# The recurrence's right-hand sides by halves of heads, its masks on an earlier signal, its group norm begun inside its last steps, and the gated merge kept in PSUM

## The reference

```python
def step(state, inp):                      # per head, per token
    r_t, w_t, k_t, v_t, kk_t, a_t = inp
    sa = jnp.einsum('bhij,bhj->bhi', state, -kk_t)
    state = (state * w_t[:, :, None, :] + sa[..., None] * (kk_t * a_t)[:, :, None, :]
             + v_t[..., None] * k_t[:, :, None, :])
    y = jnp.einsum('bhij,bhj->bhi', state, r_t)
...
mean = jnp.mean(y, -1, keepdims=True)      # group norm over each head's 64 values
var = jnp.mean(jnp.square(y - mean), -1, keepdims=True)
y = ((y - mean) * lax.rsqrt(var + LNX_EPS)).reshape(B, S, RWKV_WIDTH) * lnx_g + lnx_b
y = (y + bonus) * (jax.nn.sigmoid(gl) @ g2)
...
merged = jax.nn.sigmoid(p_ga) * (y_a @ w_up_a) + jax.nn.sigmoid(p_gb) * (y_b @ w_up_b)
h = _layer_norm(DEEPNORM_ALPHA * h + merged @ w_out, ln1_g, ln1_b)
```

## Time and profile before

| | us |
|---|---|
| runs before: median (3 runs, 3464.66 to 3469.29) | 3468.47 |
| the profiled execution's own time | 3464.38 |
| its span | 3462.6 |
| PE busy in the span | 3305.0 (95%) |
| recurrence, from the first scores' masks to the last `ry` | 1874.0 to 2009.8 |
| group norm and gates, to the first up pass | 2009.8 to 2043.9 |
| up projection, to the first pass of `s.out` | 2043.9 to 2072.6 |

### The profile page before, as it was taken

The page is one execution under the profiler, slowest core; times in us unless marked ns, Lnnn a source line. Parts: engine busy times, 40 slices in busy tenths (PEclk is TensorE's granted clock), DMA queues, the critical chain, the costliest instruction groups (busy, mean ns, idle before and its releaser), DMA issues. The chain is left out here.

```text
span 3462.6 us, 40970 instructions
## 1 busy us (share of the span) xinstructions
PE 3305.0 (95%) x17376; PEld 2653.1 (77%) x17376; DVE 1335.4 (39%) x1942; ACT 1203.5 (35%) x1816; POOL 1330.1 (38%) x555
## 2 busy tenths in 40 slices
PE   8889999999999999999999879999999999999998
PEld 6678788887687788877777757888678778878886
DVE  8963421214434411222357453001374261133733
ACT  4443422224443322234434223222344432242332
POOL 4744244444253344433252013444334324414443
PEclk9999999999999999999999989999999999999999
DMA  4232122222132222223122022222222212202231
GB/s 155 80 104 86 55 98 97 98 98 91 55 116 79 72 96 96 97 91 106 55 94 92 3 90 84 97 95 94 91 98 98 80 49 95 94 31 98 98 122 67
DMA packets 83005, 302.48 MB, mean 87 GB/s; under 512 B 9060, under 2 KB 10888, under 8 KB 81928
## 3 DMA queue, kind: packets, MB, share of 16 engines
q1 hardware_dynamic: 78368, 280.55, 24.3%
q10 hardware_dynamic: 4456, 19.33, 1.5%
HBM read 290.39 MB, written 9.44 MB: 87 GB/s over the span
## 5 line engine op out<-in xcount | busy, mean ns | idle before, releaser
L3140 POOL TENSOR_TENSOR WL<-RW,WH 128x1024 fp32r<-128x1024 f32 x527 | 1294.4, 2459 | 2105.7 <-ACT WH L269 2105.2
L274 PE MATMUL PS<-XH,WH 128*128 128x512 f32 x2968 | 1169.9, 394 | 49.3 <-DVE XL L932 15.7
L275 PE MATMUL PS<-XL,WH 128*128 128x512 f32 x2968 | 1160.6, 391 | 0.0
L276 PE MATMUL PS<-XH,WL 128*128 128x512 f32 x2968 | 1160.1, 391 | 0.0
L269 ACT ACTIVATE WH<-RW 128x1024 fp32r<-128x1024 f32 x527 | 553.6, 1053 | 804.3 <-PE PS L276 698.6
L274 PEld LDWEIGHTS PS<-XH,WH 128*128 128x128 f32 x2968 | 560.5, 189 | 186.4 <-POOL WL L3140 34.0
L276 PEld LDWEIGHTS PS<-XH,WL 128*128 128x128 f32 x2968 | 560.4, 189 | 117.6
L275 PEld LDWEIGHTS PS<-XL,WH 128*128 128x128 f32 x2968 | 560.9, 189 | 116.8 <-issue 2.2
L274 PE MATMUL PS<-YH,WH 128*128 128x512 f32 (+1 forms) x928 | 351.2, 378 | 16.1 <-POOL WL L3140 7.4
L275 PE MATMUL PS<-YL,WH 128*128 128x512 f32 (+1 forms) x928 | 349.7, 377 | 0.0
L276 PE MATMUL PS<-YH,WL 128*128 128x512 f32 (+1 forms) x928 | 349.4, 377 | 0.0
(11 more groups left out here) (523 smaller groups left out, 3115.4 us busy)
## 6 DMA issues: line engine op xcount, KB each, us to landing
RW<-in_units SPq DMA_DIRECT2D x527, 512.0 KB, 3.3
spill<-X ACTq DMA_DIRECT2D x2, 2048.0 KB, 7.4
X<-in_xT SPq DMA_DIRECT2D x8, 256.0 KB, 5.8
A<-spill ACTq DMA_DIRECT2D x1, 2048.0 KB, 7.9
X<-spill ACTq DMA_DIRECT2D x4, 512.0 KB, 6.6
X<-spill ACTq DMA_DIRECT2D x1, 2048.0 KB, 7.9
out_T<-X ACTq DMA_DIRECT2D x4, 512.0 KB, 3.0
spill<-X ACTq DMA_DIRECT2D x1, 1536.0 KB, 5.1
```

The lines of the kernel that those rows point to most:

```text
L274: mm(out, hi, xh, start=first, stop=False)
L275: mm(out, hi, xl, start=False, stop=False)
L276: return mm(out, lo, xh, start=False, stop=last)
L3140: nc.gpsimd.tensor_tensor(WL[:, u % SPLIT, :], RW[:, u % RAW, :], WH[:, u % SPLIT, :].bitcast(F32), ALU.subtract).then_inc(split_done, 1)
```

## The change

- **Right-hand sides by halves.** `b0`, `b1`, `b2` are each made and signalled as two halves of two heads, in two banks; DVE's `q0`, `q1`, `q2` become two instructions of 128 x 256 each, and the next product of a half waits for that half alone. `turn` waits by halves too.
- **Masks sooner.** The scores are written in another order, first those that `D`, `DT`, `O` and the first half of `RB` need, signalled as `ab`; the others and the transposes follow. DVE's first four masks wait for `ab`. ACT's second copy of step 1 waits for `d2t` and no longer for `w`; for this the names `D` and `K` change places.
- **`y.in` in two parts.** The half of the first chunk (`within(0)`) follows `u.mm` of the second chunk, the other half stays in step 13. `y` uses banks 3 and 1.
- **Group norm begun in the second stream's tail.** In group 1's last steps PE also makes two means and all four gate products, DVE centres two tiles and applies gain, bias and gate to them, ACT squares them. The load of the gate's weights is issued half a tile earlier.
- **The rest of the norm.** The variance is made in two pairs, between passes of gate 7; the spread factors stand between passes too. DVE multiplies in PSUM (`scaled`, `biased`), and each tile is split as soon as it is done. A small Sqrt is issued on ACT ahead of the wait for the variance.
- **Up and merge.** The first round goes tile by tile as the splits arrive. Each round signals its first half alone (`up.first`), the merged tiles stay in PSUM, and hi and lo are made from there, one tile behind. `s.out` waits for the lo parts of its banks' tiles only.

The diff, cut to its core:

```diff
-        def quarters(out, L, R, w=64):
-
-            for n in range(4):
+        def quarters(out, L, R, w=64, heads=range(4)):
+
+            for n in heads:
                 for r in halves:
...
-                            mm(o, T(j)[b, tok], AR[j][b, t, :, halves[c]], start=True, stop=True)
+                            last = mm(o, T(j)[b, tok], AR[j][b, t, :, halves[c]], start=True, stop=True)
+                st.do(last, i + ".ab")
+                for q in range(2):
+                    j = 2 * g + q
...
-                st.do(quarters(bank(B + 3), F, RHS[g], P), i + ".b0")
+                st.do(quarters(bank(B + 3), F, RHS[g], P, LOW), i + ".b0.0")
+                st.do(quarters(bank(B + 1), F, RHS[g], P, HIGH), i + ".b0.1")
...
-                st.wait(i + ".q0")
-                st.do(quarters(bank(B + 3), DT, RHS[g], P), i + ".b1")
+                st.do(quarters(bank(B), D, by_head(DT)), i + ".m2t")
+                st.wait(i + ".q0.0")
+                st.do(quarters(bank(B + 2), DT, RHS[g], P, LOW), i + ".b1.0")
+                st.wait(i + ".q0.1")
+                st.do(quarters(bank(B + 3), DT, RHS[g], P, HIGH), i + ".b1.1")
             elif step == 7:
-                st.wait(i + ".m2t_", i + ".q1")
-                st.do(quarters(bank(B + 2), K, RHS[g], P), i + ".b2")
+                st.wait(i + ".m2t_", i + ".q1.0")
+                st.do(quarters(bank(B + 1), K, RHS[g], P, LOW), i + ".b2.0")
+                st.wait(i + ".q1.1")
+                st.do(quarters(bank(B), K, RHS[g], P, HIGH), i + ".b2.1")
...
-                st.wait(i + ".q2")
                 for n in range(4):
                     w, q = n // 2, n % 2
-                    last = mm(PS[halves[w], B, q * P:(q + 1) * P], RHS[g][:, n, 0:64], ident, start=True, stop=True)
+                    if q == 0:
+                        st.wait(f"{i}.q2.{w}")
+                    last = mm(PS[halves[w], B + 2, q * P:(q + 1) * P], RHS[g][:, n, 0:64], ident, start=True, stop=True)
...
-                st.wait(i + ".w")
-                st.do(a_.activation(K, half(B + 1), ACT.Copy), i + ".d2t_")
+                st.wait(i + ".d2t")
+                st.do(a_.activation(D, half(B + 1), ACT.Copy), i + ".d2t_")
...
+                st.wait(i + ".masked")
                 st.do(a_.activation(wq(RHS[g][:, :, 0:64]), PS[:, B + 2, 256:512].rearrange("p (q w c) -> p w q c", q=2, w=2), ACT.Copy))
+                st.wait(i + ".w")
...
-                st.wait(i + ".scores")
+                st.wait(i + ".ab")
...
+                st.wait(i + ".scores")
...
             elif step == 5:
-                st.wait(i + ".b0")
-                st.do(v.tensor_copy(RHS[g], by_head(bank(B + 3))), i + ".q0")
+                for h, b in enumerate((3, 1)):
+                    st.wait(f"{i}.b0.{h}")
+                    st.do(v.tensor_copy(RHS[g][:, 2 * h:2 * h + 2, :], by_head(bank(B + b))[:, 2 * h:2 * h + 2, :]), f"{i}.q0.{h}")
...
-            if part == 4:
+
+            def within(c):
...
+            if part == 4:
+                st.do(within(1), f"y.in{t}.{g}")
...
+                if part == 2:
+                    within(0)
...
+        MEAN, GATED, SQ = (2, 0, 6, 7), (1, 3, 2, 0), (1, 2, 3, 12)
+
+        def gn_mean(st, j):
+            st.do(mm(bank(MEAN[j]), ones64, T(26 + j), start=True, stop=True), f"gn.mean{j}")
+
+        def gn_gate(st, j):
+            st.do(mm(bank(GATED[j]), T(0)[:, j * P:(j + 1) * P], T(13), start=True, stop=True), f"rw.g{j}")
...
+        def gn_early_pe(st, step):
+            if step == STATE - 1:
+                st.wait("ry3.0")
+                gn_mean(st, 0)
+            elif step == STATE:
+                gn_mean(st, 1)
+            elif step == STATE + 1:
+                st.wait("g2")
+                gn_gate(st, 0)
+            elif step == STATE + 2:
+                gn_gate(st, 1)
+            elif step == STATE + 4:
+                st.wait("gn.xc0")
+                gn_gate(st, 2)
+            elif step == STATE + 5:
+                st.wait("gn.xc1")
+                gn_gate(st, 3)
...
+        def gn_gated(st, j):
+            st.wait(f"gn.sq{j}", f"rw.g{j}", "rk.in")
+            st.settle()
+            st.do(v.scalar_tensor_tensor(out=T(18 + j), in0=T(18 + j), scalar=vec("lnx_g", j), in1=bank(GATED[j]), op0=ALU.mult, op1=ALU.mult))
+            st.do(v.scalar_tensor_tensor(out=T(30 + j), in0=T(30 + j), scalar=vec("lnx_b", j), in1=bank(GATED[j]), op0=ALU.add, op1=ALU.mult))
...
+                if (t, g, step) == (TT - 1, 0, 1):
+
+                    act.dma_start(T(0), io["lora"][:, S:2 * S]).then_inc(g2_loaded, 16)
...
+                if (t, g) == (TT - 1, 1) and step in (STATE, STATE + 1):
+                    gn_centre(st, step - STATE)
+                if (t, g, step) == (TT - 1, 1, STATE + 2):
+                    gn_gated(st, 0)
+                    gn_gated(st, 1)
...
+            gn_mean(st, 2)
+            gn_mean(st, 3)
...
+            variance(0)
+            variance(1)
+            st.wait("gn.xc2")
+            st.wait_ge(split_done, gate_unit(7) + 1)
+            for k in range(4):
+                gate(0, k)
+            variance(2)
+            st.do(variance(3), "gn.var")
+            for k in range(4, KT):
+                gate(0, k)
+            st.wait_ge(split_done, gate_unit(7) + 2)
+            for k in range(3):
+                gate(1, k)
+            st.wait("gn.inv")
+            replicate(0)
+            replicate(1)
+            gate(1, 3)
+            replicate(2)
+            gate(1, 4)
+            replicate(3)
+            for k in range(5, KT):
+                gate(1, k)
...
+            st.do(a_.activation(SD[:, 0:1], cst("one"), ACT.Sqrt))
...
+            gn_centre(st, 2)
+            gn_centre(st, 3)
+            gn_gated(st, 2)
+            gn_gated(st, 3)
...
+
+            def scaled(j):
+                st.wait(f"gn.rep{j}")
+                st.do(v.tensor_tensor(bank(j), T(18 + j), bank(j), ALU.mult))
+
+            def biased(j):
+                st.settle()
+                st.do(v.tensor_tensor(bank(j), T(30 + j), bank(j), ALU.add), f"yb.{j}")
+            scaled(0)
...
+                steps = [(n, k) for k in range(4) for n in range(2)] if r == 4 else [(n, k) for n in range(2) for k in range(4)]
+                for n, k in steps:
+                    if r == 4:
+                        st.wait(f"yb.lo{k}")
...
+                    if (n, k) == (0, 3):
+                        st.do(last, f"up.first{r}")
+                last.then_inc(unit_done, 1)
...
+                for n in range(2):
+                    k = 2 * (r - 4) + n
+                    g = SG[:, n, :] if r == 7 else X[:, k, :]
+                    st.wait(f"up.gate{r}.{n}")
+                    if n == 0:
+                        st.wait(f"up.first{r}")
+                    else:
+                        st.wait_ge(unit_done, up_unit(r) + 1)
+                    st.do(v.tensor_tensor(MERGED(k), g, MERGED(k), ALU.mult), f"ups{r}")
+                    st.settle()
+                    st.do(v.tensor_tensor(MERGED(k), T(4 + k), MERGED(k), ALU.add), f"merged.{k}")
+                    if k:
+                        split_lo_tile(st, "merged", k - 1, MERGED(k - 1), XH, XL)
+            split_lo_tile(st, "merged", 7, MERGED(7), XH, XL)
...
+            for i in range(4):
+                last = UP[0] + 28 + i
+                names[f"ev{last}"] = names[f"merged.lo{2 + last % 4}"]
+                for r in range(4, 7):
+                    names[f"ev{UP[0] + 4 * r + i}"] = names[f"ups{r}"]
```

More of the change, by code:

```diff
@@ L2546, in gn_pe, with variance, gate @@
-            st.do(last, "gn.var")
-            gates_pe(pe, st, 7)
-            st.wait("gn.inv")
-            for j in range(4):
+            gn_mean(st, 2)
+            gn_mean(st, 3)
+            def variance(j):
+                st.wait(f"gn.sq{j}")
+                return mm(PS[32 * j:32 * j + 32, 4, :], PAIRS, T(SQ[j]), start=True, stop=True)
+            def gate(n, k):
+                u, c = gate_unit(7) + n, slice(k * P, (k + 1) * P)
+                last = unit_passes(bank(GATE_BANK[7] + n), WH[:, u % SPLIT, c], WL[:, u % SPLIT, c], XH[:, k, :], XL[:, k, :], k == 0, k == KT - 1)
+                if k == KT - 1:
+                    last.then_inc(unit_done, 1)
@@ L2562, in gn_act @@
             st.do(a_.activation(SD[:], bank(4), ACT.Sqrt, bias=cst("epsx"), scale=1.0 / 64), "gn.std")
+            w_hi(act, st, gate_unit(7) + SPLIT)
+            for j in range(4):
+                st.wait(f"yb.{j}")
+                st.do(a_.activation(YH[:, 4 + j, :], bank(j), ACT.Copy), f"yb.hi{j}")
         def gn_dve(dve, st, e):
             drained(st, e)
-            for j in range(4):
-                st.wait(f"gn.mean{j}")
-                st.do(v.scalar_tensor_tensor(out=T(18 + j), in0=bank(4 + j), scalar=-1.0 / 64, in1=T(26 + j), op0=ALU.mult, op1=ALU.add), f"gn.xc{j}")
+            gn_centre(st, 2)
```

124 lines of the change are left out of this document (63 added, 61 removed).

## The result

The changed kernel takes 3433.03 us (median of four runs, 3430.68 to 3435.26) against 3468.36 (four runs, 3464.66 to 3469.29). The ratio is 0.990, with a 95% interval of 0.9883 to 0.9917. The forecast was 3434.1, range 3425 to 3446. The profiled run took 3435.26 us, of which the span is 3433.1.

What follows compares the result with a forecast made beforehand. PE, busy 95% of the span, was taken as the bound, with gains only in its waits and low clock. 13.9 - 2.9 + 15.0 + 8.4 = 34.4 us off 3464.4, plus 4.1 for the median: 3434.1, range 3425 to 3446.

Steps and rivals of the forecast that it cites:

- (a): Steady recurrence: of PE's 0.92 us before the masked products, 0.76 goes per half tile, 5.3 us in all.
- (b): Steady recurrence: PE's wait for the copy that waited for `w` goes, 0.26 us per half tile, 1.8 in all.
- (c): Steady recurrence: half of `y.in` fills the wait for `F4`, 0.3 us per half tile, 2.1 in all.
- (d): Steady recurrence: working by halves removes the wait of `b2` for `q1`, 2.9 us over seven times.
- (e): First half tile, running alone: same waits, larger, about 1.4 us; the last `q2` and `turn` give 0.4.
- The tail: Last `turn` to first mean: with six fp32 products and twelve shape changes 10.4 us against 7.55, 2.9 more.
- Norm: Group norm to first up pass: 34.1 us become 19.1, so 15.0 go; bounds 12 and 16.3.
- Up and merge: Up passes save 2.4 us, the `s.out` wait 4.3, the low clock behind it 1.7; together 8.4.
- A: Recurrence: waits only move along each group's chain, so only 7 of 13.9 us come, 3441 us; chance 0.13.
- B: Tail: clock stays low, six products cost 5.2 us more, a following stretch up to 3; 3440 to 3442; chance 0.11.
- C: Whole recurrence: granted clock falls because products are packed differently, 66 us more, 3500 us; chance 0.02.
- D: Recurrence: waits stay because another signal is later; possible for (b) alone, 2 us; chance 0.02 for almost no gain.

Runs made afterwards that it cites:

- the four undone edits: Masks after all scores, both halves waited for, copy after `w`, first half of `y.in` in step 13, against the changed kernel: 3440.48, 3438.98, 3437.09, 3431.36; together 3445.52 us.

## Why the prediction was right, and where it was off

**What bounds the kernel.** PE's waits and the low clock that follows them, as the forecast read it: PE's busy time stayed, the span fell.

**(a) Masks.** 0.76 per half tile was forecast, 0.80 measured. In the changed kernel 0.38 us from product to product remain there (start of the last of `turn` to start of `d2`), not listed as a wait.

**(b) The copy.** 0.26 was forecast, 0.46 measured. This step failed in its size: the listed wait was taken for the loss. With the 0.2 us that this wait hides, seven half tiles give 1.4 us more. It is most of what the steady part gave beyond the forecast.

**(c) `F4`.** 0.3 forecast, 0.29 measured.

**(d) Halves.** 0.41 forecast for `b2` alone, 0.37 measured for all three pairs. DVE's extra instructions (0.5 us per half tile) cost nothing measurable.

**(e) First half tile.** 1.4 forecast, 2.8 measured: 1.76 of it are the masks and 0.79 the halves, by the runs that undo them. The step failed because the first interval's waits were taken as somewhat larger ones of the steady kind; two late signals stood behind the masks there. The last `q2` and `turn`, for which 0.4 stood beside it, gave about 0.7 (2.7 from the last scores to the last `turn`, less the 2.0 of a steady half tile); no run takes it apart.

**The tail.** +2.9 forecast, +2.8 measured, with the clock at 1.00. The forecast's sum was 8.4 us of products and short steps and 2.0 for twelve changes of shape. A gate product in the tail shows both: its two records start 0.53 apart and the next product 0.52 later, 1.05 where 0.86 is the product. The sum held term by term: the short steps take 3.1 us, six products 5.15 and the gaps around them 2.0. PE's timeline there:

```profile
1996.61 1.13 PE L2528 MATMUL PS<-A 128*128 128x512 f32 x2
1997.66 0.68 PE L2450 MATMUL PS<-A 64*64 64x64 f32 x16
1998.28 1.12 PE L2528 MATMUL PS<-A 128*128 128x512 f32 x2
```

**Norm.** -15.0 forecast, -14.5 measured. Of the miss 0.3 is the price of its ten changes of shape, put at 0.13 each though the tail's were put at 0.17; the records give 1.6 us for the ten. Between the last scores and the first up pass the change gives 14.4 us (58.8 to 44.4). The early start is 4.5 of them. The run without it keeps 10.0: 3.3 up to the first mean, which are the recurrence's, and 6.7 from there to the first up pass (34.11 to 27.44). The gate's passes stood under root and reciprocal before the change too: the reciprocal ended at 2024.45 and the spread factors came at 2031.36, behind the last of the passes. New is that the spreads stand among the passes, so that DVE's factors and the splits run under PE's work, and the wait of 7.29 us ahead of the first up pass is gone. No run undoes this part by itself; PE's timeline shows it:

```profile
2010.96 1.94 PE L2631 MATMUL PS<-SD,CST 128*64 128x512 f32 x8
...
2013.73 1.08 PE L2631 MATMUL PS<-SD,CST 128*64 128x512 f32 x4
...
2015.63 1.08 PE L2631 MATMUL PS<-SD,CST 128*64 128x512 f32 x4
```

The slack was as worked out; DVE's timeline shows the reciprocal and the last lo part, which ends at 2021.2 and which PE, passing since 2018.8, needs at 2022.9:

```profile
2006.87 3.35 DVE L2676 RECIPROCAL SD<-SD 128x512 f32<-128x512 f32 x1 [2.00 <-ACT SD L2663]
2012.16 0.70 DVE L2681 TENSOR_TENSOR PS<-A,PS 128x512 f32<-128x512 f32 x1 [1.94 <-PE PS L2631]
...
2020.51 0.69 DVE L893 TENSOR_TENSOR YL<-PS,YH 128x512 fp32r<-128x512 f32 x1 [0.67 <-ACT YH L2667]
```

**Up and merge.** -8.4 forecast, -8.6 measured, and its parts, wait and clock, were reproduced by the run that brings a wait back at `s.out` (3.1 and 1.7). The 2.4 us at the low clock ahead of `s.out`'s wait, in the up passes, are read from the traces alone: 96 passes took 24.3 us before and take 21.8 now, at 1.00.

**Rivals.** A (waits only move) falls with the four undone edits, whose losses add up to the last 0.1 us. B (clock low in the tail) fell because the inserted products keep PE full; without them it is low. C fell: 1.00 in the steady part. D fell for (b), which was worth more than its listed wait. The stages gave 3.3 us more than forecast and the median came out only 1.1 below it; the 2.2 between them are within the scatter of the rest of the program.

## What to carry to other kernels

Measure what a wait on PE costs from start to start of the products around it: between short products here the listed wait was 0.2 to 0.3 us too small, and gaps of 0.28 to 0.36 weren't listed at all. Where one chain runs alone at the end of a loop, put large independent products of the next stage into its waits: here six of 0.86 us filled gaps of 3.4 us, of which 1.8 were listed, and the clock that they kept up gave 3.0 us more, for 2.0 us in the gaps around them. Put products that use different column groups of the array next to each other, and compare small variants by a stage's own length in the trace, not by medians that scatter by more.

## What the runs showed of the hardware

- A wait on PE can cost more than its listed length: listed 0.26, lost 0.46 per half tile; listed none, lost 0.37. The Trainium skill (Perfetto Trace Analysis, Tensor Engine Instruction) states that a matmul's end in the profile is an estimate and not observed. This case's trace fits: passes on the whole array, drawn 0.39 us long, start 0.23 us apart, so a drawn end isn't when the next one can start.
- Four products of 128 rows and 32 columns side by side take 0.995 us to the start of the next pass, two of them 0.98.
- A change between passes on the whole array and a product on 32 or 64 of its columns costs 0.15 to 0.17 us. A gap of 0.2 stands also between an fp32 product and a pass that both use the whole array.
- A spell of 3.4 us at 1.2 GHz costs 1.7 us of passes, behind waits of 2.96 and of 4.35 us alike; in the tail without the early start a spell of 6.8 us began behind three listed waits of 0.39 to 0.47 us and ahead of the one of 0.55, and with the early start there was none.
- The same instructions have such spells in some executions and not in others: the end part took 1293.0 to 1293.3 or 1296.8 to 1297.1 us, and nothing between.
